# A transformer block: gate columns taken into the value matmuls of the first head group

## The reference

```python
proj = h @ w_in                       # 2048 -> 2048 queries, 6 x 512 keys/values, 48 gates
kv = proj[..., qd:qd + 6 * kvd].reshape(B, S, 6, G, dh)
gates = jax.nn.sigmoid(proj[..., qd + 6 * kvd:] + b_gate).reshape(B, S, G, R, 3)
k_cmp = rms_norm(compress_kv(kv[:, :, 0], ...), k_g[0])
v_cmp = compress_kv(kv[:, :, 1], ...)
k_sel, v_sel = rms_norm(kv[:, :, 2], k_g[1]), kv[:, :, 3]
k_win, v_win = rms_norm(kv[:, :, 4], k_g[2]), kv[:, :, 5]
...
return gx[..., 0:1] * o_cmp + gx[..., 1:2] * o_sel + gx[..., 2:3] * o_win
```

## Time and profile before

| | |
|---|---|
| median of 3 runs | 2193.16 us (2191.86 to 2194.51) |
| profiled execution | span 2192.9 us from the first to the last instruction |
| busy time of PE, PEld, DVE, ACT, POOL | 2180.1, 1866.1, 1558.7, 1039.0, 101.1 us |
| mean granted clock of TensorE | 0.997 |

### The profile page before, as it was taken

One profiled execution on the slowest core, in us unless ns is written; L12 is line 12 of the kernel. 1 busy time (PEld: TensorE's weight loads), 2 busy tenths in 40 slices (PEclk: granted clock), 3 DMA queues, 4 the chain that ended last, 5 costly groups with the idle time before them and its releaser, 6 DMA issues.

```text
span 2192.9 us, 30034 instructions
## 1 busy us (share of the span) xinstructions
PE 2180.1 (99%) x11329; PEld 1866.1 (85%) x11329; DVE 1558.7 (71%) x2261; ACT 1039.0 (47%) x1482; POOL 101.1 (5%) x115
## 2 busy tenths in 40 slices
PE   9999999999999999999999999999999999999999
PEld 8898988989889998788888888888888888888887
DVE  6333466575666554798777777777877898999898
ACT  5332245343444333864445444445444565555553
POOL 1000000000001000100000000000000000000000
PEclk9999999999999999999999999999999999999999
DMA  5342212212114222654645555455465677666545
GB/s 177 116 116 87 77 59 58 68 49 67 59 58 145 68 68 78 205 169 114 181 165 154 162 164 178 122 158 183 127 175 165 183 226 239 192 196 193 173 143 165
DMA packets 209071, 300.49 MB, mean 137 GB/s; under 512 B 16588, under 2 KB 116209, under 8 KB 207521
## 3 DMA queue, kind: packets, MB, share of 16 engines
q1 hardware_dynamic: 197522, 255.40, 35.9%
q0 software_dynamic: 11408, 43.20, 9.5%
HBM read 235.35 MB, written 28.57 MB: 120 GB/s over the span
## 4 chain that ended last, share of the span: by engine, by line
PE 96%; DVE 1%; DMA 1%; ACT 1%; issue 0%; SPq 0%; DVEq 0%; ACTq 0%
PE ps L1674 93%; PE ps L2000 1%; PE ps L2070 1%; DMA g<-in_ffn_w_up_dram 0%; DMA x_rows<-in_x_dram 0%; DVE wl L1019 0%; PE ps L1976 0%; PE ps L1720 0%; PE ps L2035 0%; ACT wh L616 0%; DVE ptl L1344 0%; DVE pbuf L1321 0%; ACT left_val L865 0%; ACT pbuf L768 0%; SPq L450 0%
## 5 line engine op out<-in xcount | busy, mean ns | idle before, releaser
L616 ACT ACTIVATE wh<-g 128x1024 fp32r<-128x1024 f32 x462 | 489.9, 1061 | 581.0 <-PE ps L1674 443.2
L1019 DVE TENSOR_TENSOR wl<-g,wh 128x1024 fp32r<-128x1024 f32 x462 | 565.1, 1224 | 227.0 <-PE ps L1674 221.3
L1674 PE MATMUL ps<-wh,left_hi 128*128 128x512 f32 x1232 | 482.1, 391 | 0.9 <-DVE wl L1019 0.5
L1674 PE MATMUL ps<-wh,left_lo 128*128 128x512 f32 x1232 | 479.7, 389 | 0.0
L1674 PE MATMUL ps<-wl,left_hi 128*128 128x512 f32 x1232 | 479.4, 389 | 0.0
L1674 PEld LDWEIGHTS ps<-wh,left_hi 128*128 128x128 f32 x1232 | 231.3, 188 | 51.2 <-issue 3.5
L1674 PEld LDWEIGHTS ps<-wh,left_lo 128*128 128x128 f32 x1232 | 231.3, 188 | 48.3
L1674 PEld LDWEIGHTS ps<-wl,left_hi 128*128 128x128 f32 x1232 | 231.4, 188 | 47.0
L1674 PE MATMUL ps<-wh,down_hi 128*128 128x512 f32 x616 | 239.8, 389 | 0.0
L1674 PE MATMUL ps<-wh,down_lo 128*128 128x512 f32 x616 | 239.7, 389 | 0.0
L1674 PE MATMUL ps<-wl,down_hi 128*128 128x512 f32 x616 | 239.6, 389 | 0.0
(11 more groups left out here) (214 smaller groups left out, 2992.0 us busy)
## 6 DMA issues: line engine op xcount, KB each, us to landing
g<-in_ffn_w_gate_dram SPq DMA_DIRECT2D x176, 256.0 KB, 3.2
g<-in_ffn_w_up_dram SPq DMA_DIRECT2D x176, 256.0 KB, 4.3
g<-in_ffn_w_down_dram SPq DMA_DIRECT2D x176, 256.0 KB, 5.0
raw<-in_nsa_w_in_dram SPq DMA_DIRECT2D x164, 256.0 KB, 3.0
g<-g POOLq DMA_DIRECT2D x66, 512.0 KB, 5.0
down_val<-m_scratch SPq DMA_DIRECT2D x77, 256.0 KB, 4.5
raw<-in_nsa_w_out_dram SPq DMA_DIRECT2D x64, 256.0 KB, 3.1
m_scratch<-work SPq DMA_DIRECT2D x22, 384.0 KB, 2.9
```

The lines of the kernel that those rows point to most:

```text
L616: return nc.scalar.activation(dst, src, ACT.Copy)
L1019: nc.vector.tensor_tensor(dst, src, hi.bitcast(f32), ALU.subtract).then_inc(done, 1)
L1674: return nc.tensor.matmul(out_, a, b, start=start, stop=stop, skip_group_check=True)
```

## The change

The 48 gate columns are put behind the 256 value columns of the first group, so that one matmul makes both (304 columns). The value units become six wide units of 3, 3, 3, 3, 2 and 2 k-tiles with 304 columns each, loaded by three transfers each instead of two, and go to four banks (0 to 3, one for each tile of 128 tokens) instead of two. The two gate units, ACT's copy to `pbuf` and the four transposes are gone; DVE reads the gate sums straight from the four banks after the last wide unit. `CMP_UNITS` is 12, the `w1` units are j = 8 to 11, and `P0` stays 26.

```diff
-CMP_UNITS = 13
-P0, P_UNITS = 2 * CMP_UNITS, 16
+CMP_UNITS = 12
+V0, V_KTILES, V_COLS = 2 * CMP_UNITS, [3, 3, 3, 3, 2, 2], 2 * DH + NG
+P0, P_UNITS = V0 + len(V_KTILES) - 4, 16
...
+                    unit(V0 + s, [(dst[:, :, 0:DH], src[:, :, KVCOL[3]:KVCOL[3] + DH]),
+                                  (dst[:, :, DH:2 * DH], src[:, :, KVCOL[5]:KVCOL[5] + DH]),
+                                  (dst[:, :, 2 * DH:], src[:, :, GATECOL:GATECOL + NG])])
...
-                unit(n, k_halves(n, w_in_8[ty][:, :, GATECOL + NG - P:GATECOL + NG], 8))
...
-                    if n == CMP_UNITS + 8:
-                        act.wait_ge(units_used, n + 1)
-                        copy(pbuf[:, 0, :], bank(5)).then_inc(gateT_copied, 1)
...
+            dve.wait_ge(units_used, P0 + 4)
+            dve.wait_ge(bgate_loaded, 16)
+            nc.vector.tensor_tensor(gates[:, :, :], ps[:, 0:TT, 2 * DH:V_COLS],
...
-                    elif j == 8:
-                        for kk in range(8):
-                            k, at = 8 * ty + kk, slice(kk * P, (kk + 1) * P)
-                            last = mm3(bank(5), (wh[:, n % RING, at], wl[:, n % RING, at]), (hTh[:, k, :], hTl[:, k, :]),
-                                       k == 0, k == KD - 1)
-                        last.then_inc(units_used, 1)
                     else:
-                        if j == 9:
+                        if j == 8:
                             pe.wait_ge(c_lo, 4 * ty + 4)
                             pe.wait_ge(cols_ready, 1)
...
                     if u == 8:
-                        wait(pe, vst_ready, half + 1)
+                        wait(pe, vst_ready, 2)
+                        wait(pe, gate_arg, 1)
...
+                    for kk in range(V_KTILES[n - V0]):
+                        k, at = k0 + kk, slice(kk * V_COLS, (kk + 1) * V_COLS)
+                        last = mm3(bank(t)[:, 0:V_COLS], (hTh[:, k, ts], hTl[:, k, ts]),
+                                   (wh[:, n % RING, at], wl[:, n % RING, at]), k == 0, k == KD - 1)
...
-                if u == 2:
-                    for t in range(TT):
-                        last = nc.tensor.transpose(bank(4)[:, t * P:(t + 1) * P], pbuf[:, 0, t * P:(t + 1) * P],
-                                                   ident[:, :])
-                    last.then_inc(gates_done, 1)
```

More of the change, by code:

```diff
@@ L38, with wide_unit, unit_width, raw_count @@
 HI_RING, LO_RING = 4, 3
+def wide_unit(n):
+    return V0 <= n < V0 + len(V_KTILES)
+def unit_width(n):
+    return V_KTILES[n - V0] * V_COLS if wide_unit(n) else UNIT
+def raw_count(n):
+    return sum(48 if wide_unit(m) else 32 for m in range(n % RAW, n + 1, RAW))
 def chunk_of(t):
@@ L142 @@
 KSUM_AT, KB_AT, KB2_AT, QSUM_AT, KSPLIT_AT = 14, 18, 20, 26, STEPS - 2
+assert sum(V_KTILES) == KD and max(V_KTILES) * V_COLS <= UNIT
 assert S // SEL_BLOCK <= N_SELECT and WINDOW >= S
@@ L277, in nsa_swiglu_block @@
         rowsT_done, cols_ready, pos_hi, pos_lo = sem("rowsT_done"), sem("cols_ready"), sem("pos_hi"), sem("pos_lo")
-        gateT_copied, gates_done = sem("gateT_copied"), sem("gates_done")
         gate_arg, gate_exp, gates_ready = sem("gate_arg"), sem("gate_exp"), sem("gates_ready")
@@ L313, in nsa_swiglu_block @@
         w_in_v = w_in[0].rearrange("(q k p) c -> q p k c", k=4, p=P)
-        w_in_8 = w_in[0].rearrange("(q k p) c -> q p k c", k=8, p=P)
+        w_in_k = w_in[0].rearrange("(k p) c -> p k c", p=P)
         w_gate_v = w_gate[0].rearrange("(q k p) c -> q p k c", k=4, p=P)
@@ L393, in column_halves, with wide_units @@
                 return [(dst[:, :, 0:P], src_a), (dst[:, :, P:2 * P], src_b)]
+            def wide_units():
+                k = 0
+                for s, many in enumerate(V_KTILES):
+                    dst = raw[:, (V0 + s) % RAW, 0:many * V_COLS].rearrange("p (k c) -> p k c", k=many)
+                    src = w_in_k[:, k:k + many, :]
+                    unit(V0 + s, [(dst[:, :, 0:DH], src[:, :, KVCOL[3]:KVCOL[3] + DH]),
+                                  (dst[:, :, DH:2 * DH], src[:, :, KVCOL[5]:KVCOL[5] + DH]),
+                                  (dst[:, :, 2 * DH:], src[:, :, GATECOL:GATECOL + NG])])
+                    k += many
             def group_units(first, per, g, g1):
                 for b, (ca, cb) in enumerate(((KVCOL[3], KVCOL[5]), (KVCOL[2], KVCOL[4]))):
+                    if b == 0 and first == P0:
+                        continue
                     for q in range(4):
@@ L426, in _ @@
                         n += 1
-                unit(n, k_halves(n, w_in_8[ty][:, :, GATECOL + NG - P:GATECOL + NG], 8))
                 for j in range(4):
-                    unit(n + 1 + j, k_halves(n + 1 + j, w1_v[ty, j], 8))
+                    unit(n + j, k_halves(n + j, w1_v[ty, j], 8))
+            wide_units()
             group_units(P0, 0, 0, 0)
@@ L621, in split @@
             def split(n, per=0, i=0):
-                wait(act, raw_loaded[n % RAW], 32 * (n // RAW + 1), 32 * per // RAW, i)
+                wait(act, raw_loaded[n % RAW], raw_count(n), 32 * per // RAW, i)
                 if n >= RING:
                     wait(act, units_used, n - RING + 1, per, i)
-                copy(wh[:, n % RING, :], raw[:, n % RAW, :]).then_inc(hi_ready, 1)
+                width = unit_width(n)
+                copy(wh[:, n % RING, 0:width], raw[:, n % RAW, 0:width]).then_inc(hi_ready, 1)
             def first_squares():
@@ L711, in values_out @@
                 part_done(0, half, per, i, p)
+                if p == 0:
+                    copy(vst[:, half, :].rearrange("p (t c) -> p t c", t=2), ps[:, 2 * half:2 * half + 2, 0:2 * DH])\
+                        .then_inc(vst_ready, 1)
+                    return
                 copy(vst[:, half, :], bank(proj_bank(p, 0) + half)).then_inc(vst_ready, 1)
@@ L743, in values_split @@
                     .then_inc(v_hi, 1)
-            for u in range(P_UNITS):
+            for n in range(V0, P0 + 4):
+                if n == P0 + 3:
+                    for half in range(2):
+                        part_out(0, 0, 0, 0, half)
+                split(n + RING)
+                if n == V0 + 2:
+                    act.wait_ge(vc_done, 1)
+                    copy(vc[:, :, :].rearrange("p g d -> p (g d)"), bank(5)[0:3 * CPAD, :]).then_inc(vc_hi, 1)
+            for u in range(4, P_UNITS):
                 if u % 4 == 3:
@@ L749, in _ @@
                 split(P0 + u + RING)
-                if u == 1:
-                    act.wait_ge(vc_done, 1)
-                    copy(vc[:, :, :].rearrange("p g d -> p (g d)"), bank(5)[0:3 * CPAD, :]).then_inc(vc_hi, 1)
-                if u == 2:
+                if u == 4:
                     act.wait_ge(gate_arg, 1)
@@ L1022, in split @@
                 wait(dve, hi_ready, n + 1, per, i)
-                lo(wl[:, n % RING, :], raw[:, n % RAW, :], wh[:, n % RING, :], lo_ready)
+                width = unit_width(n)
+                lo(wl[:, n % RING, 0:width], raw[:, n % RAW, 0:width], wh[:, n % RING, 0:width], lo_ready)
             def first_denominator():
@@ L1185, in values_split @@
                    vh[:, :, :].rearrange("p t c -> p (t c)"), v_lo)
-            for u in range(P_UNITS):
+            for n in range(V0, P0 + 4):
+                split(n + RING)
+                if n == V0 + 2:
+                    dve.wait_ge(vc_hi, 1)
+                    at = vc[CPAD:2 * CPAD, :, :].rearrange("p g d -> p (g d)")
+                    lo(at, bank(5)[CPAD:2 * CPAD, :], at, vc_ready)
+            dve.wait_ge(units_used, P0 + 4)
+            dve.wait_ge(bgate_loaded, 16)
+            nc.vector.tensor_tensor(gates[:, :, :], ps[:, 0:TT, 2 * DH:V_COLS],
+                                    bgate[:, :].rearrange("p (a c) -> p a c", a=1).to_broadcast([P, TT, NG]),
+                                    ALU.add).then_inc(gate_arg, 1)
+            for u in range(4, P_UNITS):
                 if u % 4 == 3:
@@ L1200, in _ @@
                 split(P0 + u + RING)
[L1201 to L1211, removed]
+                if u == 5:
                     dve.wait_ge(gate_exp, 1)
@@ L1788, in _ @@
                         for ll in range(8):
-                            l = 8 * (j - 9) + ll
+                            l = 8 * (j - 8) + ll
                             o, e = l % CMP_STRIDE, l // CMP_STRIDE
@@ L1857, in queries_sums, with wide_values @@
                 last.then_inc(qsum_done, 1)
-            for u in range(P_UNITS):
-                if u == 1:
+            def wide_values(n, k0):
+                arrive(n)
+                for t in range(TT):
+                    ts = slice(t * P, (t + 1) * P)
+                    for kk in range(V_KTILES[n - V0]):
+                        k, at = k0 + kk, slice(kk * V_COLS, (kk + 1) * V_COLS)
+                        last = mm3(bank(t)[:, 0:V_COLS], (hTh[:, k, ts], hTl[:, k, ts]),
+                                   (wh[:, n % RING, at], wl[:, n % RING, at]), k == 0, k == KD - 1)
```

(13 more changed lines are left out.)

## The result

The kernel after takes 2215.21 us, median of 4 runs (2212.53 to 2218.25); the kernel before, beside it, 2193.05 us (2191.86 to 2194.51). The ratio is 1.0101, with a 95% interval of 1.0088 to 1.0113: one per cent slower. The profiled execution after has a span of 2211.4 us and a mean granted clock of 0.987; before it was 2192.9 us.

A forecast was written before the change was run, and what follows sets the result against it. PE was taken as the bound, busy 2180.1 of 2192.9 us. Terms of -0.45, +18.0 to 19.6 and +3.2 to 5.0 summed to +20.7 to +24.2 us, middle 2215.6 us; range 2195.5 to 2220 us.

The forecast's parts named there:

- Wider value matmuls: Value units: 192 matmuls grow by 48 columns, 20 ns each, for +3.84 us.
- Gate units and the wait that they hid: Behind column unit 7: 48 matmuls go, -10.9 us, but PE waits 3.5 us twice for cbl, leaving -3.85 us.
- The time of the fall: At each cbl wait: the clock falls between 0.4 us before PE resumes and 0.9 us after.
- The `w1` stretch: Behind each wait: 88 to 96 of 96 matmuls at +102 ns, 18.0 to 19.6 us for both.
- The tail: Large matmuls behind each w1 stretch: 3.4 to 5.4 us at the lower clock, +3.2 to +5.0 us for both.
- Loads, key units, GELU: Wide-unit loads, the values' copy, bias and exponential before the key units, and the GELU wait before w2: hidden, 0 us.
- the comparison of the span with the median: Whole kernel before: its profiled span of 2192.9 us was taken as 0.3 us under the median of 2193.16.
- comes back within the `w1` stretch: Rival, w1 units: the clock falls but recovers there, 1.6 us lost per wait, 2196.0 us; chance 0.13.
- no fall: Rival, at the two cbl waits: the clock stays up, sum -0.45 us, 2192.7 us; chance 0.09.
- faster: Rival, behind column unit 7: cbl wait met without a stall, -7.5 us, 2185.7 us; chance 0.03.
- no wide load was late: Denies a rival at ty 1's w1 units: wide loads one unit late, up to 5 us more, 2221 us; chance 0.03.

The follow-up runs named there:

- the third: The kernel before with its gate unit moved behind the wait for cbl instead of ahead of it; 2205.64 us, ratio 1.0059.
- the fourth: The kernel after with ACT's copy of the third bank released after the first half of column unit 7; 2212.39 us, ratio 1.0086 to the kernel before.
- the reordered kernel: The kernel after with the first ty 1 column unit and first wide unit put in the gate units' places; 2187.69 us, ratio 0.998 to the kernel before.

## Why the prediction was right

The forecast was 2215.6 us, and the time is 2215.21: slower, by the mechanism named, a wait behind which the clock falls and does not come back in the `w1` stretch. By its steps:

- **Wider value matmuls, +3.8 us**: right. From 162.28 to 165.78 lie 25 steps of 140 ns.
- **Gate units and the wait that they hid**: right. PE stands from 67.79 to 71.23 and from 136.11 (227 ns after the last column matmul) to 139.55, 3.44 us each, against 3.51 and 3.50. The wait that had long been met came last once its cover was gone.
- **The time of the fall**: 1.4 us after PE goes on, later than the 0.9 us given; about 12 of the 96 matmuls still ran at full clock. Nor is it fixed: over the experiments it lies between the end of the wait (the third, second wait) and 2.6 us behind it (the fourth, second wait).
- **The `w1` stretch, +18.0 to 19.6 us**: 8.61 + 8.66 = 17.3 us, for that reason. The 102 ns a matmul are right.
- **The tail, +3.2 to 5.0 us**: mis-sized. The clock was back 2.6 and 2.4 us into the large matmuls instead of 3.4 to 5.4. In the first, 2.6 us at 427 instead of 227 ns a matmul lose 1.2 us, in the second 2.4 us at 254 instead of 140 ns lose 1.1: 2.3 us.
- **Loads, key units, GELU, at nothing**: right. From 158.88 to 187.73 PE has no wait; apart from those 1.1 us this stretch runs at its pitch.

Together: -10.88 + 6.88 + 3.84 - 0.44 + 17.3 + 2.3 = +19.0 us, which is what the stage measured. The prediction's sum was +20.7 to 24.2, too high by the two terms above.

That the median still fell on the forecast is partly luck, and the step was the comparison of the span with the median. A run's time after lies 1.9 to 2.1 us above its span (2213.33 against 2211.4 us in the profiled execution). If that holds for the profiled execution of before, whose own time is not on record, it was, with its 2192.9, not 0.3 us under the median but some 1.8 us over it; that of after was 1.9 us under its own. The 18.5 us between the spans and these 3.7 make the 22.2 between the medians. The runs of one kernel differ in granted clock as well: after, 2212.53 us at 0.988 and 2218.25 at 0.985. In the profiles there are short falls of the clock in the attention, as in the earlier trace rows, that differ from one kernel's profile to the next: after, there are three, at 271, 554 and 687 us. The clocks on record fit the 2.3 us missing in the medians of the reordered kernel: its eleven runs have a mean granted clock of 0.9958, the fourteen of before beside them 0.9970, and 0.0012 of 2188 us is, as an estimate, 2.6 us of full clock. In which stretches those runs lost it is not shown, as one run of each kernel was profiled.

Of the rivals, "comes back within the `w1` stretch" was refuted by the windows at 0.50; "no fall" too, since the clock fell behind both waits, and behind waits of even 2.32 us; "faster" needed the wait covered, and the reordered kernel shows its number; no wide load was late.

## What to carry to other kernels

Before removing work from a bound engine, ask which waits it covers, and look at what follows them: here a 3.4 us wait cost 13 us, since the work behind it was of a kind that does not bring the clock back. Put useful large matmuls in the place of what is removed; if there are none, large matmuls that nobody reads are better than standing still (2193.0 against 2215.2 us); small ones are not (2213.8). In the profile, compare the pitch of equal matmuls and the granted clock of a stretch, as a busy share of 100% hides a halved clock.

## What was not expected of the hardware

- The same 96 matmuls of 128 columns have two lasting speeds: 10.60 us at a clock of 1.00 when they begin and stay at it, and 19.3 us when the clock falls near their start. They hold the higher clock and, in the 18 us of the stretch, do not win it back. The prediction took it so; no row of before had shown it.
- The clock fell with PE busy all the time on matmuls of 32 columns, 3.50 us long.
- After the change the clock is still granted in full at the end of each wait of 3.4 us and falls 1.4 us into the work behind it, so the slow stretch begins where PE is already busy again.
